# Operand buffers of a feed-forward stage moved to other byte places in SBUF

## The reference

```python
h = rms_norm(x, norm_mix);  proj = h @ w_in + b_in            # 31 tiles of 128 columns
o_a = nsa_attention(...);   o_b = swa_sink_attention(...)      # 16 + 16 heads of 64
x = x + concatenate([o_a, o_b]) @ w_out
h = rms_norm(x, norm_ffn)
x = x + (silu(h @ w_gate) * (h @ w_up)) @ w_down
return rms_norm(x, norm_final)
```

## Time and profile before

| | us |
|---|---|
| median of 3 runs | 2102.66 |
| all runs | 2099.91, 2102.66, 2113.5 |
| the profiled execution, time | 2099.91 |
| the profiled execution, span of its instructions | 2098.2 |
| mean granted TensorE clock | 0.990 |

### The profile page before, as it was taken

One profiled execution on the slowest core, in us unless ns is written; L12 is line 12 of the kernel. 1 busy time (PEld: TensorE's weight loads), 2 busy tenths in 40 slices (PEclk: granted clock), 3 DMA queues, 4 the chain that ended last, 5 costly groups with the idle time before them and its releaser, 6 DMA issues.

```text
span 2098.2 us, 32169 instructions
## 1 busy us (share of the span) xinstructions
PE 2040.7 (97%) x13205; PEld 1817.0 (87%) x13205; DVE 1566.1 (75%) x2106; ACT 956.3 (46%) x1476; POOL 277.1 (13%) x153
## 2 busy tenths in 40 slices
PE   8999999999979999999999999999999999999998
PEld 6888777777658889999999999999999988888886
DVE  6723566777762227888898889889888898988995
ACT  5222356667652227544444444444444433333343
POOL 4000011211120000123113203203203100000002
PEclk9999999999989999999999999999999999999999
DMA  7671222211035334335446445345345755665622
GB/s 262 217 208 61 61 66 56 61 56 53 13 121 186 115 121 140 102 131 179 154 141 198 134 159 192 122 157 185 131 147 186 301 194 188 228 213 181 236 106 81
DMA packets 197779, 306.46 MB, mean 146 GB/s; under 512 B 8640, under 2 KB 121344, under 8 KB 192512
## 3 DMA queue, kind: packets, MB, share of 16 engines
q1 hardware_dynamic: 197600, 304.38, 43.6%
q10 hardware_dynamic: 32, 0.01, 0.0%
HBM read 248.79 MB, written 55.57 MB: 145 GB/s over the span
## 4 chain that ended last, share of the span: by engine, by line
PE 88%; DVE 6%; issue 3%; ACT 2%; DMA 0%; POOL 0%; DVEq 0%; ACTq 0%; POOLq 0%
PE bank L2641 11%; PE bank L2644 11%; PE bank L2646 11%; PE bank L2698 6%; PE bank L2696 6%; PE bank L2693 6%; PE bank L2242 3%; PE bank L2244 3%; PE bank L2243 3%; PE bank L2508 3%; PE bank L2510 3%; PE bank L2512 3%; PE bank L2408 3%; PE bank L2530 2%; PE bank L2534 2%
## 5 line engine op out<-in xcount | busy, mean ns | idle before, releaser
L1297 ACT ACTIVATE w_all<-raw 128x1024 fp32r<-128x1024 f32 x292 | 305.6, 1058 | 279.6 <-PE bank L2698 156.9
L1891 DVE TENSOR_TENSOR w_all<-raw,w_all 128x1024 fp32r<-128x1024 f32 x292 | 378.0, 1306 | 71.5 <-ACT w_all L1297 71.0
L2641 PE MATMUL bank<-x_T,w_all 128*128 128x256 f32 x1344 | 373.2, 278 | 0.0
L2646 PE MATMUL bank<-x_T,w_all 128*128 128x256 f32 x1344 | 373.2, 278 | 0.0
L2644 PE MATMUL bank<-x_T,w_all 128*128 128x256 f32 x1344 | 373.2, 278 | 0.0
L2641 PE MATMUL bank<-x_B,w_all 128*128 128x256 f32 x1008 | 280.9, 279 | 0.8 <-DVE w_all L1891 0.2
L2644 PE MATMUL bank<-x_B,w_all 128*128 128x256 f32 x1008 | 279.9, 278 | 0.0
L2646 PE MATMUL bank<-x_B,w_all 128*128 128x256 f32 x1008 | 279.9, 278 | 0.0
L2641 PEld LDWEIGHTS bank<-x_T,w_all 128*128 128x128 f32 x1344 | 254.2, 189 | 0.0
L2644 PEld LDWEIGHTS bank<-x_T,w_all 128*128 128x128 f32 x1344 | 252.3, 188 | 0.0
L2646 PEld LDWEIGHTS bank<-x_T,w_all 128*128 128x128 f32 x1344 | 252.3, 188 | 0.0
(11 more groups left out here) (299 smaller groups left out, 4394.3 us busy)
## 6 DMA issues: line engine op xcount, KB each, us to landing
raw<-in_w_gate SPq DMA_DIRECT2D x39, 1024.0 KB, 5.1
h_scratch<-late SPq DMA_DIRECT2D x70, 512.0 KB, 3.1
raw<-in_w_down SPq DMA_DIRECT2D x50, 512.0 KB, 5.2
proj_q<-in_w_up SPq DMA_DIRECT2D x22, 1024.0 KB, 6.8
raw<-in_w_up SPq DMA_DIRECT2D x22, 1024.0 KB, 7.9
x_B<-h_scratch SPq DMA_DIRECT2D x20, 1024.0 KB, 5.0
raw<-in_w_in SPq DMA_DIRECT2D x16, 1024.0 KB, 10.4
raw<-in_w_out SPq DMA_DIRECT2D x16, 1024.0 KB, 5.5
```

The source lines that it names most:

```text
L1297: nc.scalar.activation(piece_hi(p), piece_raw(n, k), ACT.Copy).then_inc(piece_hi_done, 1)
L1891: nc.vector.tensor_tensor(piece_lo(p), piece_raw(n, k), piece_hi(p).bitcast(F32), ALU.subtract).then_inc(piece_lo_done, 1)
L2641: nc.tensor.matmul(dst, wh[:, t, cs], x_lo(x)[:, cols], start=start and part == 0 and t == 0 and a == 0, stop=False, skip_group_check=True)
L2646: done = nc.tensor.matmul(dst, wh[:, t, cs], x_hi(x)[:, cols], start=False, stop=part == 1 and t == 3, skip_group_check=True)
```

## The change

No instruction is added, removed, reordered or made longer or shorter. The buffers lose the 512 bytes of padding and the offset of 48 elements, and instead an unused tensor of its own length (`X_GAP`, in bytes) is allocated ahead of each. Every reader and writer of a buffer (operands of gate and up, h, sums, last weights) now uses the same start. Worked out from the sizes, bytes per partition past a multiple of 512:

| buffer | first byte, before | operands of gate and up, before | h, sums, last weights, before | first byte, after | everything, after |
|---|---|---|---|---|---|
| T2 | 109696 | 320 | 128 | 109952 | 384 |
| T3 | 126592 | 320 | 128 | 126624 | 160 |
| T4 | 143488 | 320 | 128 | 143168 | 320 |
| B22 | 160384 | 320 | 128 | 159968 | 224 |
| T1 | 177280 | 320 | 128 | 176832 | 192 |
| B21 | 194176 | 320 | 128 | 193280 | 256 |
| B11 | 211072 | 320 | 128 | 210048 | 128 |

```diff
         x_names = sorted(X_PLACE, key=X_PLACE.get)
-        X_SIZE = 2 * HALF_KT * HALF_TOK
-        X_AT = dict.fromkeys(x_names, 48)
+        X_GAP = {"T2": 256, "T3": 288, "T4": 160, "B22": 416, "T1": 480, "B21": 64, "B11": 384}
+        x_plain, xc = {}, {}
         with ExitStack() as plain:
-            x_plain = {name: plain.enter_context(nc.sbuf_tensor(
-                f"x_plain_{name}", [P, X_SIZE + 128], F32)) for name in x_names}
-        xc = {name: sb(f"x_{name}", [P, X_SIZE + 128], F32R) for name in x_names}
-
-        def half_of(buf, name, half, at):
-            size = X_SIZE // 2
-            return buf[name][:, at + size * half:at + size * (half + 1)]
-
+            for name in x_names:
+                plain.enter_context(nc.sbuf_tensor(f"gap_{name}", [P, X_GAP[name] // 4], F32))
+                x_plain[name] = plain.enter_context(nc.sbuf_tensor(
+                    f"x_plain_{name}", [P, 2, HALF_KT * HALF_TOK], F32))
+        for name in x_names:
+            sb(f"space_{name}", [P, X_GAP[name] // 4])
+            xc[name] = sb(f"x_{name}", [P, 2, HALF_KT * HALF_TOK], F32R)
...
         def x_hi(name):
-            return half_of(xc, name, 0, X_AT[name])
+            return xc[name][:, 0, :]
 
         def x_lo(name):
-            return half_of(xc, name, 1, X_AT[name])
+            return xc[name][:, 1, :]
...
-            return half_of(x_plain, where, half, X_AT[where])
+            return x_plain[where][:, half, :]
...
         def h_flat(r):
-            return half_of(xc, H_HOME[r][0], H_HOME[r][1], 0)
+            return xc[H_HOME[r][0]][:, H_HOME[r][1], :]
...
         def sums(name, half):
-            return half_of(x_plain, name, half, 0).rearrange("p (q i c) -> p q i c", q=2, i=2)
+            return x_plain[name][:, half, :].rearrange("p (q i c) -> p q i c", q=2, i=2)
...
-        last_lo = [half_of(xc, "T4", 1, 0), h_flat(1), h_flat(3), h_flat(5)]
+        last_lo = [xc["T4"][:, 1, :], h_flat(1), h_flat(3), h_flat(5)]
```

More of the change, by code:

```diff
@@ L424, in build @@
         x2_last = work[:, :].rearrange("p (i c) -> p i c", i=TT)
-        x2_junk = [x_plain[name][:, UNIT_COLS * n:UNIT_COLS * (n + 1)]
+        x2_junk = [x_plain[name][:, :, :].rearrange("p h (n c) -> p (h n) c", c=UNIT_COLS)[:, n, :]
                    for name in ("T1", "B21") for n in range(8)]
         def x_hi(name):
-            return half_of(xc, name, 0, X_AT[name])
+            return xc[name][:, 0, :]
         def x_lo(name):
-            return half_of(xc, name, 1, X_AT[name])
+            return xc[name][:, 1, :]
         def x_full(name):
@@ L494, in sums @@
         def sums(name, half):
-            return half_of(x_plain, name, half, 0).rearrange("p (q i c) -> p q i c", q=2, i=2)
+            return x_plain[name][:, half, :].rearrange("p (q i c) -> p q i c", q=2, i=2)
         sum_11, sum_7, sum_3 = sums("T2", 1), sums("T3", 0), sums("T3", 1)
         sum_4, sum_u, sum_5 = sums("B22", 0), sums("B22", 1), sums("T4", 0)
-        y_junk = half_of(x_plain, "T2", 0, 0)
+        y_junk = x_plain["T2"][:, 0, :]
         y_rows = [[sum_11, sum_3], [sum_4, sum_7]]
```

## The result

The changed kernel takes 2130.87 us (median of 6 runs, 2128.86 to 2133.18). The kernel before takes 2111.52 us in the six runs beside it (2099.91 to 2115.97). The ratio is 1.0102, with a 95% interval of 1.0084 to 1.012: slower by 1.0%, where I had forecast 2104 us and no change. Two things strike at once. The time lies above the upper end of my range (2122). And the scatter is much smaller: the runs of before spread over 16 us, those of the changed kernel over 4.

What follows compares the result with a forecast made beforehand. TensorE's matmul start rate was taken as the bound. From the profiled 2099.9 us, +4 for gate and up's pace and 0 each for weight loads, other engines and DMA gave 2104 us; range 2089 to 2122 us.

Steps and rivals of the forecast that it cites:

- The bound and the two paces: Gate and up: TensorE's matmul rate bounds the kernel; spacing is 113.3 ns or 117.8 ns, changing only at stops.
- the moving operand's term: Gate and up, 7440 matmuls: the moving operand's place has no part in the pace; bounds -10.4 to +18.6 us.
- the draw: Gate and up: chance at stops decides the pace; turning slow one or two periods earlier adds 4 us.
- The upper bound: Gate and up all at 117.8 ns, less 8 stops: +18.6 us, 2118.5 us.
- the slow pace of before: Gate and up: spacing of 117.8 ns, seen for 2642 of 7440 matmuls, taken as the dearest case.
- rival 3: Gate and up: T3 and B22, 32 past a multiple of 64, cost 4.5 ns beyond 117.8; 2127 us, chance 0.14.
- Rival 2: Gate and up: the new places hold 117.8 ns; 2118.5 us, about 2117 with T4 left free; chance 0.20.
- My reason against a third pace: Gate and up: no operand at any place shows a spacing other than 113.3 and 117.8 ns.
- The weight loads' term: Down product, h loaded as weights from moved places: 0 us, with +8.4 us kept for the rivals.
- DVE's, ACT's and the sums' durations: Additions and copies on the moved buffers: durations unchanged, 0 us.
- the loads of h: DMA, 35 loads of 1 MB: double the time would still be hidden, 0 us.
- The weighed rule: Gate and up: warm matmuls start 109.2 ns apart for 256 columns; placement could give back 4.1 ns or more each.

Runs made afterwards that it cites:

- the kernel at 320: Kernel before with all seven gate and up operands at distance 320 bytes (moving less stationary start, modulo 512): 2120.85 us, ratio 1.0038.
- the isolated half of the change: Kernel before with only h, the sums and the last weights moved to the changed kernel's places: 2121.05 us, ratio 1.0047.

## Why the prediction was wrong, by its steps

**The bound and the two paces** held. TensorE's rate is what the time is made of, and within the kernel before the pace turned only at stops, in both profiles with all operands at 192.

**The step that failed is the moving operand's term.** From "within either pace all seven operands go at one rate" I took that the place has no part, though I noted that all seven share their place within 512 bytes and that the row therefore says nothing about other places. The forecast rested on just what the rows could not show. What the runs showed in its place: the distance to the stationary operand sets the pace, together with what the stream did before. Measured for the changed kernel over groups 1 to 21 are 834.8 us for 7056 matmuls, 118.3 ns; at 117.8 ns (the kernel at 320) it is 831.4. Of the 27.0 us between the forecast's 2103.9 and 2130.9, 19.4 are the places, of which 6.9 in the down product and its last block; both terms stood at 0 in the sum. The other 7.6 are the draw.

**The upper bound was no bound.** I took the slow pace of before as the dearest. B11, T2 and B22 cost 120. The condition named for rival 3 was the wrong one too: of the two buffers at 32 past a multiple of 64, T3 (distance 32) is one of the cheaper at 117.7 and B22 costs 120.1, but so do B11 and T2 at multiples of 64. Rival 2 with a piece of rival 3 is what happened: a stream held at about 118, and a little more. (Rival 2's 2117 with T4 left free was also mis-added: T4's 1008 matmuls at 4.5 ns are 4.5 us, so a fast T4 would have made it 2114.) My reason against a third pace, that no operand had shown one, was the same reading of one place as if it were all.

**The weight loads' term was 0 and measured 6.1 us** in the down product and 0.8 in the last block. I had 8.4 as the upper bound and left it to the rivals; the isolated half of the change gave 6.8 (4 to 16). My ground was that 512 columns return to one pace by themselves. They do so at distance 0, the only one that these matmuls have in before.

**The draw was mis-sized.** I added 4 us to the profiled run; before's median beside the changed kernel is 2111.5, so 11.6 above it, and beside this study's kernels 2112.8 to 2115.6, so 13 to 16 above. Every profile has a stop in group 2 or 4 at either pace, but a stream that is slow after group 4 was seen to meet no further one, so it stays slow. That most runs turn slow early fits their times and is not shown, since only one run of before was profiled. Two of the three runs shown (2099.9 and 2102.7) were lucky ones.

The account against a kernel that is always slow closes: the kernel at 320 takes 2120.85 us; groups 1 to 21 of the changed one take 834.8 - 831.4 = 3.4 us more, the first group 0.6, the down product and last block 6.9; sum 2131.8, measured 2130.87, within the scatter of either. The rest of the loss against before, 2120.85 - 2111.52 = 9.3 us, I put down to the fast stretches that its runs had.

**What cost nothing, as forecast:** DVE's, ACT's and the sums' durations, and the loads of h, which land in 4.8 and 7.6 us (5.0 and 7.7) with no wait of TensorE.

**The weighed rule and the two reads.** The rule that I had weighed, in the Trainium skill 2.5 ns above N / 2.4 GHz, "TensorE: Matmul & The Clock Gate", section "Wait — 56ns, not 53.3ns?", was not reached in any run: 113.3 ns is the least of 22 distances, 6.6 above 106.7. The Trainium skill, "SBUF — State Buffer", section "Who interferes with whom", says that TensorE has two independent read ports, one for the moving operand and one for the weights. The runs disagree in effect: moving the weights by 64 bytes, with the moving operands at the same place modulo 512, changed the spacing from 113.3 or 117.8 to 118.7 or 120.0 ns. What in the hardware does it, whether the two reads meet somewhere, was not tested and stays open, as does why 16 and 272 lead into the slow pace and 96, 128, 208 and 240 into the fast one.

## What to carry to other kernels

When a stream of matmuls is the bound, read its spacing from the start times, operand by operand, and treat the distance in bytes between the stationary and the moving operand as a tuning parameter; scan it with one operand at each distance in a single run, since one profile shows them all, and then try the good ones again behind another neighbour, since an operand's pace also depends on the one before it. A time that scatters by most of a per cent from run to run can be one stream with two steady paces: look for where it turns before comparing medians of a few runs. And where all rows of a trace share one value of the thing that a change alters, they bound nothing; the range has to say so.

## What the runs showed of the hardware

- The spacing of fp32r matmuls of 256 columns depends on the distance modulo 512 bytes: 113.3 to 120.2 ns at the same granted clock of 1.00, up to 6%. With 512 columns it was 226.7 ns at distances 0 and 256 and 229.2 to 234.6 at 32, 64, 96, 128, 160 and 192 (here stationary less moving).
- At distances 192, 320 and 448 there are two steady paces, 113.3 and 117.8 ns, and at 128 two others, 118.7 and 120.0. At 192 a stop that puts 0.38 us between two starts turned the fast pace into the slow one, and one of 0.48 us the slow into the fast; smaller ones turned it too (one spacing of 0.21 us at 192, two of 0.22 us at 128). At 320 some 6600 matmuls went by without a turn when nothing stopped them.
- An operand of 48 matmuls at another distance decides which of the two the next one, at 192, falls into, in all 21 groups of each kernel that had it: 208, 96, 128 and 240 into the fast one, 16 into the slow one. From 288 into 320 it was the fast one in 18 of 21. Sixteen bytes on one half of one operand, without any other change, gave 0.7%, and the runs scattered over 6 us where those of before beside them scattered over 30.
